# Modulation vectors on VectorE beside two products, and the first layer's output, norm and queries tile by tile

## The chip, the core and the metric

The kernel runs on one core of a Trainium2 chip, as one program. The metric is device time in microseconds (us); the time before is the median of three runs. Within the core TensorE (PE) multiplies matrices into PSUM, VectorE (DVE), ScalarE (ACT) and GpSimd (POOL) work on SBUF and PSUM, and SyncE (SP) issues loads. Every engine runs its own queue in order; they wait for each other on semaphores. Sixteen DMA engines carry all transfers of the core.

## The reference

All values are float32. There are 256 tokens of width 1024, in two tiles of 128. A first block has two layers, each a mixer, an output product with residual and norm, and a feed-forward part that fetches 128 experts a token (8 heads, 16 each). A second block has two layers, each with a modulation vector.

```python
# first block, layer i
x = layer_norm(DN_ALPHA * x + mix @ w_out[i], ln1_g[i], ln1_b[i])
q = x @ peer_w_q[i]                       # 8 heads, 2 halves of 128
s = q . subkeys                           # 128 keys a half, top 16 of each, top 16 of the 256 sums
y = sum over the 16 chosen experts of 8 heads: softmax(sums) * gelu(u_tab[e] . x) * v_tab[e]
x = layer_norm(DN_ALPHA * x + y, ln2_g[i], ln2_b[i])
# second block
c_act = silu(c)
for l in range(2):
    mod = c_act @ w_ada[l] + b_ada[l]     # 1024 -> 3072
    shift, scale, gate = split(mod, 3)
    h = rms_norm(x, norm_g[l]) * (1 + scale) + shift
    x = x + gate * (attention_parts(h @ w_in[l]) @ w_o[l])
```

## The kernel before

**Weights.** All large weights pass through a ring of three slots (`RING = 3`). SyncE issues the loads in the order in which `weights.add` was called (L2730); load n waits until half 1 of product n-3 is done (`half_done[1]`). A group of 512 columns is two DMAs of 1.05 MB. A product's two halves go to the PSUM banks `bank(slot, half)` and wait for `bank_read` of the product that used them before.

**Stages.** Code is cut into stages; `meet` drains TensorE, ScalarE and VectorE and lets each wait for the others.

**The first layer** (`mlstm_layer`). One stage makes the gate, memory and query/key products on TensorE (`qk`, four groups of 384 columns) while VectorE runs the gates: `log1p_steps`, the scans, `exp_reduce`. After cross-attention the decay stage follows: for each of 4 heads TensorE makes scores, VectorE the decay exponents, ScalarE the exponentials. Layer 0's modulation vector is made in this stage on TensorE: `partial_sums` (L855) multiplies a group of w_ada with silu(c) in four column groups, ScalarE copies the partial sums, `full_sum` adds them by ones and adds the bias (L869, L870), ScalarE copies the row. Then come the normalised output `ro`, `residual_product` with w_out for both tiles (L302, L936), `layer_norm_stage` for both tiles and `x_transposes`, each a stage of its own.

**The expert stream** (`middle`). A table of slots sets the order: 4 tiles (2 layers of 2) of 128 slots. A slot is one gather of 128 expert rows of 8 KB (L2361, GpSimd), one dot product (L1864, VectorE), its gelu, coefficient and diagonal (ScalarE, by pairs), and one addition on TensorE (L1758, eight instructions). Eight rows are in flight: gather n waits for addition n-8. Everything else is placed between slots by numbers that `beside()` yields: on TensorE the queries of heads 4 to 7, the memory products, layer 1's modulation vector (slots 62 to 106, w_ada's six groups), and layer 1's mixer; on VectorE the ranking of the chosen experts in pieces (`route`), which `plan_chunk` places. Ahead of slot 0 stand the queries of heads 0 to 3 (`queries(0, h)`, 256 columns, both tiles at once), the key products, the ranking of head 0 and most of head 1's. `order` and `homes` give every side job its PSUM bank.

**After the stream**, in its last stage, `second_layer(0)` makes `rv_`, `rz`, `rq` and `rk` from w_in, ten groups of 512 columns, and goes on to the attention.

Of the kernel before, what the change touches and what calls it, by code (L numbers as in the profile page):

```python
# [169 lines left out]
def program(nc, a, out, parts=None):  # L170
# [27 lines left out]
    c_col = sb([P, KD], name="silu_c")  # L198
    c_wide = sb([P, KD, 32], name="silu_c_and_zeros")
# [46 lines left out]
    norm_loaded, rg_loaded = sig("norm_gain_and_shift_landed"), sig("gate_matrices_landed")  # L246
    mod_cols_in, sums_read = sig("modulation_columns_landed"), sig("expert_sums_read")
# [243 lines left out]
    def load_mod_cols(act):  # L491

        act.wait_ge(mod_stored.sem, 16 * DEPTH)
        with nc.allow_non_contiguous_dma("small parameters"):
            for layer in range(DEPTH):
                act.dma_start(mod_cols[:, layer, 0, :], a["norm_g_2"][layer].rearrange("(k p) -> p k", p=P))\
                    .then_inc(mod_cols_in.sem, 16)
                for i in range(2):
                    act.dma_start(mod_cols[:, layer, 1 + i, :],
                                  a["mod_scratch"][layer][i * D:(i + 1) * D].rearrange("(k p) -> p k", p=P))\  # L500
                        .then_inc(mod_cols_in.sem, 16)

    def mod_gains(dve):

        dve.wait_ge(mod_cols_in.sem, 16 * 3 * DEPTH)
        for layer in range(DEPTH):
            chains["vector"](dve.scalar_tensor_tensor(
                out=mod_cols[:, layer, 0, :], in0=mod_cols[:, layer, 2, :], scalar=1.0, in1=mod_cols[:, layer, 0, :],
                op0=ALU.add, op1=ALU.mult))
# [238 lines left out]
    def setup_pool(pool):  # L748
# [7 lines left out]
        p(pool.memset(c_wide[:, :, :], 0.0))  # L756
# [21 lines left out]
    def setup_scalar(act):  # L778
# [4 lines left out]
        act.activation(c_wide[:, :, 0], c_col[:, :], ACT.Silu)  # L783
# [41 lines left out]
    class Modulation:  # L825


        def __init__(self, layer):
            self.layer = layer
            self.row = sb([1, 3 * D], name="mod_row")  # L830
            self.part = sb([P, 2, 512], name="mod_partial")
# [5 lines left out]
        def add_weights(self):  # L837
            self.run = weights.add([(a["w_ada_2"][self.layer], 0, P, KD)], 0, 512, 6)

        def place(self, g):  # L840
            n = self.run.first + g
            return n, n % RING, n // RING

        def partial_sums(self, pe, g):
            n, slot, turn = self.place(g)
            w = weights.view(slot, KD, 512)

            pe.wait_ge(landed[slot].sem, (turn + 1) * 32)
            if g >= 1:
                before, s, t = self.place(g - 1)  # L850

                pe.wait_ge(bank_read[s][0].sem, t + 1)
            for k in range(KD):
                j = k % 4
                last = pe.matmul(psum[32 * j:32 * j + 32, 6, :], c_wide[:, k, :], w[:, k, :], start=k < 4, stop=k >= 4)  # L855
            last.then_inc(half_done[0].sem, 1)

        def full_sum(self, pe, g):
            n, slot, turn = self.place(g)

            pe.wait_ge(bank_read[slot][0].sem, turn + 1)
            if g >= 1:
                before, s, t = self.place(g - 1)

                pe.wait_ge(bank_read[s][1].sem, t + 1)
            else:

                pe.wait_ge(bias_landed.sem, self.need)
            pe.matmul(psum[0:1, 7, :], ones[:, 0:1], self.part[:, g % 2, :], start=True, stop=False)  # L869
            pe.matmul(psum[0:1, 7, :], ones[0:1, 0:1], self.row[:, g * 512:(g + 1) * 512], start=False, stop=True)\  # L870
                .then_inc(half_done[1].sem, 1)
# [336 lines left out]
    def middle():  # L1208
# [567 lines left out]
        def vector(dve):  # L1776
# [298 lines left out]
            for _ in experts_norm(5, 3, 0):  # L2075
                pass
# [724 lines left out]
```

## Time and profile before

| | |
|---|---|
| median of 3 runs | 2686.25 us (2684.17 to 2686.85) |
| the profiled execution | 2687.56 us, span 2685.7 us |
| mean granted clock of TensorE | 0.885 |
| busy: PE, DVE, ACT, POOL | 78%, 50%, 27%, 22% of the span |
| read from HBM | 745.64 MB |
| first gather, last gather issued | 285.00, 1769.57 us |

The busy shares are means over parts with different limits, so they say little by themselves. The page's slices (67 us each) show the parts, and the timeline gives start, length, engine, line and tiles, with the idle time before a row and what ended it in brackets. "x16" is a number of instructions; a float32 product on TensorE is two. A window row gives its length, the busy time of each engine with its instructions, the granted clock (1.00 is 2.4 GHz, 0.50 is 1.2 GHz), the mean busy share of the DMA engines and GB/s; with a line as filter only that line's engine is shown.

### The profile page before, as it was taken

What the parts mean: (1) busy time and instruction counts of PE and PEld (TensorE: products, weight loads), DVE (VectorE), ACT (ScalarE), POOL (GpSimd) and SP (SyncE); (2) the same over time, 40 slices, a digit from 0 to 9 for tenths busy, and PEclk for the clock granted to TensorE, in tenths of its full rate; (3) what the DMA queues carried; (4) which work ended last, traced back from release to release, by engine and by line L of the source; (5) the groups of instructions that cost most, each with busy time, mean ns of one, the idle gap of its engine ahead of it and who ended that gap; (6) DMA issues with size and microseconds to landing.
All of it is one profiled execution on the core that took longest, in us unless ns stands there. A gap on an engine that the chain in (4) does not pass through costs nothing. (4 is left out here: it accounts for less than half of the span.)

```text
span 2685.7 us, 29026 instructions
## 1 busy us (share of the span) xinstructions
PE 2084.0 (78%) x10382; PEld 1082.4 (40%) x10382; DVE 1344.5 (50%) x3611; ACT 730.7 (27%) x2078; POOL 590.3 (22%) x530
## 2 busy tenths in 40 slices
PE   7987777676676776677685456669998999999897
PEld 5644423111243342243251111126864544875553
DVE  3143686666778546787556867540024322012432
ACT  0120233233335322344323233320032410022230
POOL 0000344334433433334333344510000000000000
PEclk9999899777887898888797788779999999999899
DMA  5354799999999999999998999974413143430331
GB/s 174 133 204 145 291 416 419 420 418 417 416 380 392 409 419 416 367 387 399 414 420 343 391 402 421 421 317 157 151 38 135 35 157 131 151 120 29 119 115 63
DMA packets 209159, 748.67 MB, mean 279 GB/s; under 512 B 29764, under 2 KB 69700, under 8 KB 143476
## 3 DMA queue, kind: packets, MB, share of 16 engines
q0 software_dynamic: 73728, 536.90, 48.9%
q1 hardware_dynamic: 111120, 195.35, 20.5%
q10 hardware_dynamic: 24168, 14.57, 1.9%
q8 instruction: 83, 1.36, 0.2%
q14 instruction: 60, 0.49, 0.0%
HBM read 745.64 MB, written 1.12 MB: 278 GB/s over the span
## 5 line engine op out<-in xcount | busy, mean ns | idle before, releaser
L1758 PE MATMUL psum<-expert_rows,coefs_on_diagonal 64*64 64x512 f32 x4096 | 660.3, 751 | 486.5 <-ACT coefs_on_diagonal L2145 486.1
L2361 POOL DMA_INDIRECT expert_rows<-in_peer_uv,expert_ids x512 | 585.5, 1144 | 1179.0 <-PE psum L1758 859.9
L1864 DVE SCALAR_TENSOR_TENSOR expert_rows<-expert_rows,x 128x1024 f32<-128x1024 f32 x512 | 626.5, 1225 | 412.5 <-DMA expert_rows<-in_peer_uv,expert_ids 407.7
L1758 PEld LDWEIGHTS psum<-expert_rows,coefs_on_diagonal 64*64 64x64 f32 x4096 | 141.7, 155 | 835.2 <-ACT coefs_on_diagonal L2145 655.3
L2135 ACT ACTIVATE gelu_dots<-dots 128x2 f32<-128x2 f32 x256 | 52.0, 203 | 939.7 <-DVE expert_rows L1864 900.9
L302 PE MATMUL psum<-xT,ring 128*128 128x256 f32 (+2 forms) x1088 | 237.2, 381 | 2.1 <-DVE bias_rows L715 2.1
L575 PE MATMUL psum<-ring,xT 128*128 128x512 f32 (+2 forms) x448 | 217.6, 585 | 0.0
L302 PEld LDWEIGHTS psum<-xT,ring 128*128 128x128 f32 (+2 forms) x1088 | 196.6, 181 | 44.3 <-DVE bias_rows L715 3.7
L2145 ACT ACTIVATE coefs_on_diagonal<-ident,coefs 128x128 f32<-128x128 f32 x512 | 177.5, 393 | 8.4
L1465 PEld LDWEIGHTS psum<-xT,ring 128*128 128x128 f32 x768 | 109.3, 197 | 84.4 <-issue 79.2
L1465 PE MATMUL psum<-xT,ring 128*128 128x128 f32 (+1 forms) x768 | 142.4, 330 | 0.6 <-DVEq L2705 0.6
L2138 ACT ACTIVATE coefs<-gelu_dots,gate_weights 128x1 f32<-128x1 f32 x512 | 123.0, 287 | 8.5
L664 ACT ACTIVATE prob<-soft,small 128x128 f32<-128x128 f32 (+1 forms) x96 | 53.9, 561 | 170.4 <-DVE small L632 154.8
L2410 PE MATMUL psum<-ring,xT 128*128 128x512 f32 x192 | 86.2, 610 | 7.8 <-DVE x L1897 4.1
L575 PEld LDWEIGHTS psum<-ring,xT 128*128 128x128 f32 x448 | 72.8, 194 | 29.5 <-issue 21.3
L302 PE MATMUL psum<-ring,xT 128*128 128x512 f32 (+1 forms) x192 | 78.4, 568 | 5.2 <-DVE num L1144 3.3
L1559 PEld LDWEIGHTS psum<-xT,ring 128*96 128x96 f32 x512 | 59.2, 167 | 41.3 <-issue 41.3
L1559 PE MATMUL psum<-xT,ring 128*96 128x128 f32 x512 | 69.7, 286 | 0.0
L2410 PEld LDWEIGHTS psum<-ring,xT 128*128 128x128 f32 x192 | 37.3, 196 | 55.8 <-issue 51.7
L2458 DVE SCALAR_TENSOR_TENSOR ya<-psum,small,silu_az 128x64 f32<-128x64 f32 x32 | 9.1, 284 | 98.0 <-PE psum L587 98.0
L2640 PE MATMUL psum<-ring,mergedT 128*128 128x512 f32 x128 | 55.6, 594 | 2.8 <-DVEq L2705 1.4
L2438 DVE COPY da_qT<-psum 128x512 f32<-128x512 f32 x6 | 4.1, 691 | 106.2 <-PE psum L302 106.2
(449 smaller groups left out, 2284.5 us busy)
## 6 DMA issues: line engine op xcount, KB each, us to landing
ring<-in_w_in SPq DMA_DIRECT2D x64, 1024.0 KB, 7.1
ring<-in_w_ada SPq DMA_DIRECT2D x24, 1024.0 KB, 12.7
ring<-in_peer_w_q SPq DMA_DIRECT2D x24, 1024.0 KB, 28.5
ring<-in_mlstm_w_in SPq DMA_DIRECT2D x16, 768.0 KB, 5.1
ring<-in_rglru_w_in SPq DMA_DIRECT2D x16, 768.0 KB, 26.4
expert_rows<-in_peer_uv,expert_ids POOLq DMA_INDIRECT x512, 14.4
ring<-in_w_out_b SPq DMA_DIRECT2D x8, 1024.0 KB, 7.2
ring<-in_w_o SPq DMA_DIRECT2D x8, 1024.0 KB, 5.9
```

The lines of the kernel that those rows point to most:

```text
L302: last = pe.matmul(o, l, r, start=first, stop=end)
L575: ins = pe.matmul(o, l, r, start=first, stop=end)
L664: act.activation(prob[:, j % 2, 0:w], soft[:, j % 2, 0:w], ACT.Exp, bias=small[:, 0, at4(j)], accum_out=small[:, 1, at4(j)]).then_inc(expe ...
L1465: last = pe.matmul(out[:, s * wide:(s + 1) * wide], w[:, kt, at:at + P], right[:, kt, :], start=kt == 0, stop=kt == KD - 1)
L1559: last = pe.matmul(out[0:RG_B, b * P:(b + 1) * P], w[:, kt, at:at + RG_B], xT[:, kt, t * P:(t + 1) * P], start=kt == 0, stop=kt == KD - 1)
L1758: last = pe.matmul(psum[64 * half:64 * half + 64, 2 * t + m, :], diag[tokens, n % DIAGS, tokens], rows[tokens, at_, D + half * 512:D + (ha ...
L1864: dve.scalar_tensor_tensor(out=rows[:, at_, 0:D], in0=rows[:, at_, 0:D], scalar=1.0, in1=x[:, n // TILE % NT, :], op0=ALU.mult, op1=ALU.mu ...
L2138: ins = act.activation(coef[:, at_ + q:at_ + q + 1], gel[:, at_ + q:at_ + q + 1], ACT.Copy, scale=gw[:, g_at:g_at + 1])
L2145: ins = act.activation(diag[:, (s + q) % DIAGS, :], ident[:, :], ACT.Copy, scale=coef[:, at_ + q:at_ + q + 1])
L2361: pool_.indirect_dma_start(out=rows[:, n % ROWS, :], out_offset=None, in_=table, in_offset=bass.IndirectOffsetOnAxis(ap=ids[:, at_:at_ + 1 ...
L2410: last = pe.matmul(o, l, r, start=first, stop=end)
L2640: last = pe.matmul(o, l, r, start=first, stop=end)
```

## The change

Modulation is no longer made by products on TensorE. `multiply` lets VectorE take a group of w_ada from the ring: a `tensor_scalar` for k = 0 and seven `scalar_tensor_tensor`, each adding `w[:, k, :] * silu(c)[:, k]` to `acc` [128, 512]. `reduce` adds the 128 partitions of `acc` on TensorE with a column of ones, in two products of 256 columns, and `add_bias` adds the row on VectorE. Layer 0's six groups move from the decay stage into the query/key stage, one between every two of its products. Layer 1's six groups leave the stream and stand between the six `rq` and `rk` groups of the stage after it. `load_mod_cols` and `mod_gains` are done for each layer apart.

The output product of the first layer, its norm, and the transposes now are part of the stream's stage. `out_product(pe, t)` makes both groups of w_out for one tile. VectorE adds the residual and norms tile 0 while TensorE makes tile 1's product. `queries(0, h)` for both tiles become `pair_queries(c, t)`: two heads of one tile, four blocks of 128 columns in one bank. Ahead of slot 0 stand tile 0's heads 0 to 3; tile 1's x is turned at slot 0, and the other six pairs follow in slots 4 to 45, five matmuls a slot.

Cut to its core, the diff:

```diff
@@ Modulation
+        def multiply(self, dve, g):
...
+            dve.wait_ge(landed[n % RING].sem, (n // RING + 1) * 32)
+            if g >= 2:
+
+                dve.wait_ge(half_done[1].sem, self.at[g - 2] + 1)
+            v(dve.tensor_scalar(acc, w[:, 0, :], c_act[:, 0:1], None, ALU.mult))
+            for k in range(1, KD):
+                ins = dve.scalar_tensor_tensor(out=acc, in0=w[:, k, :], scalar=c_act[:, k:k + 1], in1=acc,
+                                               op0=ALU.mult, op1=ALU.add)
...
+        def reduce(self, pe, g):
...
+            pe.wait_ge(mod_summed.sem, self.first + g + 1)
+            for half in range(2):
+                if n >= RING:
+
+                    pe.wait_ge(bank_read[n % RING][half].sem, n // RING)
+                pe.matmul(bank(n % RING, half)[0:1, 0:256], ones[:, 0:1], self.acc[:, g % 2, half * 256:half * 256 + 256],
+                          start=True, stop=True).then_inc(half_done[half].sem, 1)
@@ mlstm_layer, tensor
+            mod.reduce(pe, 0)
+            product(pe, kvj)
+            for i in range(4):
+                mod.reduce(pe, i + 1)
+                product(pe, [(qk[i], "features", x_k, [(0, 0, 0, 96), (0, T, 96, 96), (1, 0, 192, 96), (1, T, 288, 96)])])
+            mod.reduce(pe, 5)
@@ mlstm_layer, vector
             v(dve.tensor_tensor(lf[:, :], z[:, :], lf[:, :], ALU.subtract))
+            mod.multiply(dve, 2)
+            mod.add_bias(dve, 1)
@@ decay stage
-                for g in mod_groups[h]:
-                    mod.partial_sums(pe, g)
-                    mod.full_sum(pe, g)
@@ end of the first layer
-        residual_product([(a["w_out"][layer], 0, P, KD)], 512, lambda k: mixT[:, k, :])
-        layer_norm_stage(gain, shift, dict(scalar=lambda act: act.wait_ge(mod_stored.sem, mod.stored)))
-        x_transposes()
@@ middle, tensor ahead of slot 0
-            all_of(queries(0, 0))
+            out_product(pe, 0)
...
-            second = queries(0, 1)
+            out_product(pe, 1)
+            turn_x(0)
+            x_read(0)
+            out_read(pe)
+            all_of(pair_queries(0, 0, (0, 1), ("q0",)))
+            second = pair_queries(0, 0, (2, 3))
...
-            all_of(queries(0, 2))
-            all_of(queries(0, 3))
+            all_of(pair_queries(1, 0))
@@ middle, tensor beside()
-                for g in range(6):
-                    yield 62 + 8 * g
-                    partial_modulation(g)
-                    yield 66 + 8 * g
-                    full_modulation(g)
@@ middle, vector ahead of the ranking
+            for t in range(NT):
+                for g in range(2):
+                    residual(dve, g, t)
+                    norm_stats(t, g)
...
+                for _ in norm(t, t, 0):
+                    pass
@@ second_layer
+            for i, (run, dst, first) in enumerate(rqk):
+                if mod:
+                    mod.reduce(pe, i)
+                product(pe, [(run, "features", x_k, four)])
```

How the change moves instructions, at three places.

TensorE in the query/key stage, before (`xT` is the layer's input turned, `memT` the memory, `ring` the weights):

```order
L302 MATMUL psum<-xT_69,ring_67 128x256 x16
L302 MATMUL psum<-memT_70,ring_67 128x256 x16
L302 MATMUL psum<-ring_67,memT_70 128x256 x16
L302 MATMUL psum<-xT_69,ring_67 96x256 x128
L560 MATMUL psum<-kmT_99,xqT_98 128x256 x2
```

and now:

```order
L303 MATMUL psum<-xT_69,ring_67 128x256 x16
L867 MATMUL psum<-mod_partial_sums_112,ones_50 1x256 x2
L303 MATMUL psum<-memT_70,ring_67 128x256 x16
L303 MATMUL psum<-ring_67,memT_70 128x256 x16
L867 MATMUL psum<-mod_partial_sums_112,ones_50 1x256 x2
L303 MATMUL psum<-xT_69,ring_67 96x256 x32
L867 MATMUL psum<-mod_partial_sums_112,ones_50 1x256 x2
L303 MATMUL psum<-xT_69,ring_67 96x256 x32
```

The `reduce` products stand between the groups, and what follows each on TensorE waits behind it.

TensorE from the output product to slot 0, before (`mixT` is the mixer's output turned, `peer_qT` the queries):

```order
L302 MATMUL psum<-ring_67,mixT_125 128x512 x32
L336 MATMUL psum<-ident_49,x_68 128x128 x16
L1465 MATMUL psum<-xT_69,ring_67 128x256 x16
L1729 MATMUL psum<-ident_49,subkeys 128x128 x4
L1465 MATMUL psum<-xT_69,ring_67 128x256 x4
L1519 MATMUL psum<-subkeysT_152,peer_qT_153 128x128 x2
L1465 MATMUL psum<-xT_69,ring_67 128x256 x12
L1519 MATMUL psum<-subkeysT_152,peer_qT_153 128x128 x2
L1465 MATMUL psum<-xT_69,ring_67 128x256 x32
```

and now:

```order
L1211 MATMUL psum<-ring_67,mixT 128x512 x16
L1756 MATMUL psum<-ident_49,subkeys 128x128 x4
L1211 MATMUL psum<-ring_67,mixT 128x512 x16
L1561 MATMUL psum<-ident_49,x_68 128x128 x8
L1516 MATMUL psum<-xT_69,ring_67 128x128 x20
L1549 MATMUL psum<-subkeysT_143,peer_qT_144 128x128 x2
L1516 MATMUL psum<-xT_69,ring_67 128x128 x12
L1549 MATMUL psum<-subkeysT_143,peer_qT_144 128x128 x2
L1516 MATMUL psum<-xT_69,ring_67 128x128 x32
```

Ahead of the first key product there are now 8 transposes and 20 products of 128 columns, where there were 16 and 20 of 256.

VectorE in the query/key stage behind the gates' log (`log_f`), where before `cum_f` followed at once, now:

```order
L1012 TENSOR_TENSOR log_f_92<-ml_z_90,log_f_92 4x256
L850 TENSOR_SCALAR mod_partial_sums_112<-ring_67,silu_c_57 128x512
L852 SCALAR_TENSOR_TENSOR mod_partial_sums_112<-ring_67,silu_c_57,mod_partial_sums_112 128x512 x7
L882 TENSOR_TENSOR mod_row_111<-mod_row_111,psum 1x256 x2
L1015 SCALAR_TENSOR_TENSOR cum_f_93<-ones_50,log_f_92 4x256
L1016 TENSOR_TENSOR a_94<-gate_i_87,cum_f_93 4x256
```

Group 2's multiplication and the bias row of group 1 stand between two steps of the gates.

## Rows read from the trace of the kernel before

Timeline rows: start in us, length in us, engine, line, operation, written tile, read tiles, shapes, number of instructions, and in brackets the idle time before and what ended it. Window rows: stretch, length, busy time of each engine shown (with its instructions), granted clock, DMA share, GB/s.

**Rows 1.** Page, part 2: DMA engines, 40 slices, busy tenths
```profile
DMA  5354799999999999999998999974413143430331
```

**Rows 2.** Windows of the gathers' line (slots 48 to 111; 432 to 495)
```profile
411.30:607.60 196.30, 69.83 (x64) 0.78 1.02 419
...
1573.90:1734.40 160.50, 75.92 (x64) 0.78 1.01 421
```

**Rows 3.** Timeline of SyncE: start, length, engine, line, operation, tiles
```profile
418.25 74.92 SPq L2730 DMA_DIRECT2D ring<-in_w_ada  x8
...
517.67 27.45 SPq L2730 DMA_DIRECT2D ring<-in_w_ada  x4
...
568.00 177.39 SPq L2730 DMA_DIRECT2D ring<-in_rglru_w_in  x10
```

**Rows 4.** Timeline, query/key stage and its end
```profile
54.67 55.42 PE L302 MATMUL psum<-xT,ring 128*96 128x256 f32 x256
...
65.50 0.68 DVE L1005 TENSOR_TENSOR_SCAN cum_f<-ones,log_f 4x256 f32<-4x256 f32 x1
...
110.79 1.13 PE L560 MATMUL psum<-kmT,xqT 64*128 64x256 f32 x4 [0.71 <-ACTq L2705]
```

**Rows 5.** Timeline, decay stage and the stage behind it
```profile
146.74 2.93 PE L1072 MATMUL psum<-qkT 96*128 96x256 f32 x8 [0.51 <-DVEq L2705]
...
149.47 0.56 DVE L356 SCALAR_TENSOR_TENSOR decay_t<-decay_turns,decay_t 128x384 f32<-128x384 f32 x1
...
150.73 0.86 DVE L1085 SCALAR_TENSOR_TENSOR decay_t<-psum,a_and_floor_columns,causal_t 128x256 f32<-128x256 f32 x2
...
153.08 1.02 PE L869 MATMUL psum<-mod_partial,ones 128*1 128x512 f32 x2 [0.72 <-ACT mod_partial L880]
...
154.03 1.01 PE L870 MATMUL psum<-mod_row,ones 1*1 1x512 f32 x2
...
156.04 0.87 DVE L1085 SCALAR_TENSOR_TENSOR decay_t<-psum,a_and_floor_columns,causal_t 128x256 f32<-128x256 f32 x2
...
183.38 4.19 PE L1126 MATMUL psum<-v_and_ones,p_t 128*128 128x193 f32 x24 [1.21 <-ACTq L2705]
```

**Rows 6.** Timeline, output product and the first query read
```profile
217.81 27.73 PE L302 MATMUL psum<-ring,mixT 128*128 128x512 f32 x64 [1.42 <-ACTq L2705]
...
271.59 0.59 ACT L2091 COPY peer_qT<-psum 128x512 f32<-128x512 f32 x1 [20.04 <-issue]
```

**Rows 7.** Timeline, first ranking to gather 8
```profile
273.44 0.29 DVE L1797 MAX8 best_scores<-key_scores 128x8 f32<-128x128 f32 x1 [4.52 <-ACT key_scores L2105]
...
285.00 1.09 POOL L2361 DMA_INDIRECT expert_rows<-in_peer_uv,expert_ids  x1 [278.33 <-DVE expert_ids L1838]
...
296.06 0.18 DVE L1852 TENSOR_TENSOR gate_exp<-gate_exp,gate_power 128x16 f32<-128x16 f32 x1 [10.44 <-ACT gate_exp L364]
...
305.63 1.22 DVE L1864 SCALAR_TENSOR_TENSOR expert_rows<-expert_rows,x 128x1024 f32<-128x1024 f32 x1
...
311.33 3.69 PE L1758 MATMUL psum<-expert_rows,coefs_on_diagonal 64*64 64x512 f32 x16 [15.22 <-ACT coefs_on_diagonal L2145]
...
313.62 1.64 POOL L2361 DMA_INDIRECT expert_rows<-in_peer_uv,expert_ids  x1 [18.84 <-PE psum L1758]
```

**Rows 8.** Windows at the stream's start
```profile
285.00:320.00 35.00, 19.05 (x95) 11.94 (x93) 21.28 (x68) 11.05 (x30) 12.05 (x12) 0.76 0.80 312
...
310.00:315.00 5.00, 3.67 (x17) 0.85 (x17) 4.80 (x15) 3.53 (x14) 1.38 (x1) 0.50 0.13 45
```

**Rows 9.** Timeline of TensorE in tile 1: six products, one addition (8 instructions)
```profile
961.12 1.60 PE L1465 MATMUL psum<-xT,ring 128*128 128x128 f32 x12
...
963.93 1.09 PE L1758 MATMUL psum<-expert_rows,coefs_on_diagonal 64*64 64x512 f32 x8 [1.21 <-ACT coefs_on_diagonal L2145]
```

**Rows 10.** Stage after the stream: TensorE's timeline, and a window
```profile
1856.00 83.04 PE L302 MATMUL psum<-xT,ring 128*128 128x256 f32 x384
...
1856.00:1864.00 8.00, 8.00 (x39) 7.04 (x38) 0.00 (x0) 1.18 (x2) 0.00 (x0) 1.00 0.74 262
```

More of the change, by code:

```diff
@@ L837, in add_weights @@
         def add_weights(self):
[L838 to L871, printed above, removed]
+            g = len(self.at)
@@ L874, in load_bias, with add_bias @@
             act.dma_start(self.row[:, :], row(a["b_ada_2"][self.layer], 1, 3 * D)).then_inc(bias_landed.sem, 16)
-        def read_partial(self, act, g):
-            n, slot, turn = self.place(g)
-            act.wait_ge(half_done[0].sem, n + 1)
-            act.copy(self.part[:, g % 2, :], psum[:, 6, :]).then_inc(bank_read[slot][0].sem, 1)
-        def read_sum(self, act, g):
-            n, slot, turn = self.place(g)
-            act.wait_ge(half_done[1].sem, n + 1)
-            act.copy(self.row[:, g * 512:(g + 1) * 512], psum[0:1, 7, :]).then_inc(bank_read[slot][1].sem, 1)
+        def add_bias(self, dve, g):
+            n = self.at[g]
+            if g == 0:
+                dve.wait_ge(bias_landed.sem, self.need)
+            for half in range(2):
+                dve.wait_ge(half_done[half].sem, n + 1)
+                cols = slice(g * 512 + half * 256, g * 512 + half * 256 + 256)
+                dve.tensor_tensor(self.row[:, cols], self.row[:, cols], bank(n % RING, half)[0:1, 0:256], ALU.add)\
+                    .then_inc(bank_read[n % RING][half].sem, 1)
@@ L997, in vector @@
             exp_reduce(dve, v, e[:, :], gkf[:, :], gki[:, :]).then_inc(to_act.sem, 1)
+            mod.multiply(dve, 1)
+            mod.add_bias(dve, 0)
             kv_dve(dve)
@@ L1033, in scalar @@
             exp_rest(act, c, z2[:, :]).then_inc(to_dve.sem, 1)
-            read_both(act, qk, lambda g, half, b: act.copy(qkT[:, bass.ds(g * 4 + 2 * half, 2), :], two(b, 96)))
+            for i in range(4):
+                read_both(act, qk[i], lambda g, half, b, i=i: act.copy(qkT[:, 4 * i + 2 * half:4 * i + 2 * half + 2, :],
+                                                                       two(b, 96)))
+            mod.store(act)
         stage(tensor=tensor, vector=vector, scalar=scalar)
@@ L2387, in second_layer @@
         rz = weights.add([(w, 0, P, KD)], 4608, 512, 1)
-        rq = weights.add([(w, 0, P, KD)], 0, 512, 3)
-        rk = weights.add([(w, 0, P, KD)], 1536, 512, 3)
+        mod = None
+        if layer == 0:
+            attend_at, place[0] = place[0], ya_end + 8 * 1024
+            mod = Modulation(1)
+            place[0] = attend_at
+        rqk = []
+        for i in range(6):
+            if mod:
+                mod.add_weights()
+            rqk.append((weights.add([(w, 0, P, KD)], i * 512, 512, 1), qT if i < 3 else kT, i % 3 * 4))
         x_k = lambda k: xT[:, k, :]
@@ L2422, in scalar @@
             read_both(act, rz, lambda g, t, b: act.activation(az[:, t, :], b, ACT.Silu))
-            for run, dst in ((rq, qT), (rk, kT)):
-                read_out(act, 0, run, lambda g, b: act.copy(dst[:, bass.ds(g * 4, 2), :], two(b)))
+            for run, dst, first in rqk:
+                read_out(act, 0, run, lambda g, b: act.copy(dst[:, first:first + 2, :], two(b)))
+            if mod:
+                mod.store(act)
+                load_mod_cols(act, 1)
         turned_at = 4 * layer
```

328 lines of the change are left out of this document (180 added, 148 removed).

## The prediction

> **What bounds the kernel now.** I read the page's slices first: from slice 6 to slice 26 of 40 the DMA row stands at 9, and outside that stretch it is mostly at 5 or below [rows 1]. So the program has three parts with two bounds: before the expert stream TensorE and its waits, in the stream the 16 DMA engines, after it TensorE again. Next I counted gathers: 64 of them took 196.3 us in slots 48 to 111 and 160.5 us in slots 432 to 495, at the same granted clock (0.78) and the same DMA share [rows 2]. The reader is to see that no engine's instructions set this pace: what differs is what else the DMA engines carry. In the slow stretch they carry the 12 loads of w_ada, 1.05 MB each [rows 3].
>
> **Stream without w_ada.** The excess is 196.3 - 160.5 = 35.8 us. The first two of the next row, 1.05 MB together, fall there too, so w_ada's part is 12.58 / 13.63 of it: 33.0 us. Bounds: 12.58 MB at 421 GB/s [rows 2] is 29.9 us; the whole excess is 35.8. I take 33. TensorE's modulation products go with it, but nothing waited on them there.
>
> **Modulation of layer 0, in the query/key stage.** TensorE runs 256 matmuls from 54.67 to 110.09 without a gap, and the next stage starts at 110.79 [rows 4]. Now six `reduce` steps stand between its products, two 256-column products of one row each. The nearest rows are the 512-column ones, which start 0.95 us apart [rows 5]; two of half the width: 0.95 us a step, 5.7 us in all. VectorE multiplies before each step: one tensor_scalar and seven scalar_tensor_tensor over 512 columns. The row for 384 columns is 0.56 us at a pitch of 0.59 [rows 5]; scaled to 512 with the fixed part kept it is 0.69 at 0.72, so one group costs 7 x 0.72 + 0.45 = 5.5 us (the tensor_scalar is an estimate, bounds 0.3 and 0.72). Is it in time? Walking the order with these durations: group 0 is multiplied while TensorE is still in the stage's first product. TensorE wants it at 40.9 (54.67 less two memory products of 6.9). Group 1's load is let go by `reduce` 0 at 42 behind 1 MB of memory values, lands near 50.5, is multiplied by 56, its bank is freed by `add_bias` 0 (two instructions of about 0.4 us) at 56.8: 0.8 us late. Group 2 stands behind the log1p polynomial, which in the trace ends before the scan at 65.50 [rows 4] and now ends 2.5 us later; 68.0 + 5.5 = 73.5 against 71.7: 1.8 us late. Groups 3 to 5 each have a product of 13.8 us in front of them and need 8 us for the load and 5.5 for the multiply: in time. At the end `add_bias` and the store are 1.2 us longer than the copy they replace. Sum +9.5 us; bounds +5.7 (nothing late) and +14.
>
> **Layer 0's decay stage loses its modulation.** It lasts from 146.74 until TensorE's next stage at 183.38 [rows 5]. What is left is VectorE's chain: one head every 156.04 - 150.73 = 5.3 us where modulation doesn't hold it. Four heads and the last wait for ScalarE end near 168.5, the next stage at 169.4: -14.0 us (bounds -12 and -15). ScalarE now also waits for the row's store there, issued some 25 us before.
>
> So the output product of layer 0, at S = 217.81 before [rows 6], starts at about 213.3.
>
> **Output, norm and queries by tile.** Before: product 27.7 us, norm, transposes, `q` of head 0, a wait for ScalarE, which issued parameter loads and could read that `q` only at 271.59, key product, ranking from 273.44 = S + 55.6, first gather at 285.00 = S + 67.2 [rows 6, 7]. After: tile 0 is normed beside tile 1's product. S + 28.3 product and transposes of keys done; tile 0's x turned by S + 30.2; ScalarE's copies come behind `root(1)`, S + 31.8; 16 products of 128 columns S + 35.4; copy, key product, copy: ranking from S + 37.7. VectorE has finished tile 1's norm at S + 33.7. First gather S + 49.3: -17.9 us. Where a stall goes, what is late next? VectorE's wait for `gate_exp`, 10.4 us at 296.06 [rows 7]: in ScalarE's queue it stood behind two full query reads. Now one read stands there (S + 48), before VectorE asks at S + 50. So the first dot moves from S + 87.8 [rows 7] to S + 61.7, and gather 8, which needs the first addition, from S + 95.8 to S + 69.7. The eight gathers ahead occupy DMA 8 x 2.5 = 20 us from S + 49.3, so no hole is left; before, DMA was idle 20% of 285 to 320 = 7.0 us, most of it after 310 [rows 8]. -7.0 us (bounds -4 and -7).
>
> What this moves into the saturated stretch: the fourth group of peer_w_q (2.1 MB), earlier loaded before the first gather, now released in slot 11; at 33.0 / 12.58 = 2.62 us per MB, +5.5. The gain and shift of ln2, 1.05 MB, now loaded at slot 80: +2.6 (at 2.39 to 2.62 per MB).
>
> TensorE in slots 4 to 45: per slot now 4.6 products of 128 columns instead of 2 of 256. Six cost 1.60 us, an addition 1.09 [rows 9], so 1.2 to 1.35 + 1.05 = 2.3 to 2.4 us against DMA's 2.51 per slot. Nearly bound; I put 3 us for it (bounds 0 and 12).
>
> **Modulation of layer 1, in the first stage after the stream.** TensorE is gapless there [rows 10]; six steps of 0.95 add 5.7, the store and column loads fit behind the last half product of 6.9 us: +6 (bounds +5.5 and +12). The margin: a group of 2.1 MB is in within 8 us of its release [rows 10] (262 GB/s x 8 us), plus 5.5 us is 13.5, and 14.8 are there. Behind the waiting `reduce` stands the next query/key product and the rest of the stage.
>
> **Sum** against the profiled execution's 2687.56: +9.5 - 14.0 - 17.9 - 7.0 - 33.0 + 5.5 + 2.6 + 3 + 6 = -45.3. The small column loads, three of six, leave the stream: -1 to -3, I take 1.5. Total -46.8: 2640.8. The median of the runs shown is 1.3 below the profiled execution: **2639.5 us**.
>
> **Rivals.** (A) Late multiplications; the one that ends slower. Place: `reduce` 3 to 5 of layer 0 and 1 to 5 of layer 1, with a group's load sharing the DMA engines with the one issued 1 us behind it. Both then land only after 4.2 MB, some 12.5 us: 18 against 14.8, 3.2 us late at each of 8 steps, 26 us. It becomes slower than before only if each wait also lets TensorE's clock fall: after its wait before 311.33 the granted clock was 0.50 (1.2 GHz) and 16 instructions took 3.69 us instead of 2.1 [rows 7 to 9]. A product of 13.8 us half of it at this clock costs 6.9 more, 8 x 6.9 = 55: 2639.5 + 26 + 55 = 2720. It decides from where load plus multiply exceeds 14.8 us by enough to drop the clock; against it, the wait in the row was 15.22 us, not 3, and the margin is positive. 4%. The Trainium skill (TensorE: Matmul & The Clock Gate, section "HAM oscillation — how this bites in real kernels") speaks for it: it tells of a kernel in which every short wait for a load makes the next products start on the low clock. It also says, in DMA: Bandwidth & Descriptors, section "Queues, rings and completion order", that the descriptors that SyncE issues are taken in ring order on each DMA engine, by which the second load would not delay the first and the stall would be nothing. No row of before has two such loads close together, so none shows which holds.
> (B) TensorE sets the pace in slots 4 to 45: 2.8 us a slot in place of 2.51 is 12 us, so 2639.5 + 9 = 2649, up to 2655. For it: 2.3 to 2.4 is close, and additions come in pairs; against it, in the trace TensorE makes up such slots in the next ones while rows are still queued. 16%.
> (C) The stream doesn't give back the bytes: slots 48 to 111 were slow because ranking and landing latency (eight rows in flight) set the pace. Then about half of 33 us stays: 2656. Against it: same clock and share in both rows [rows 2]. 7%.
> (D) All bounds on the good side, and w_ada worth 35.8: 2630. 9%.
> The forecast itself, 2631 to 2649: 64%.
>
> **Range and chances.** 8 in 10 is held by the forecast, D's upper part and most of B: 2627 to 2656. A measurement of this kernel tells about 0.2% (5 us) from no change. Only A, with 4%, is slower; no change would need several misses at once, 1%; faster 95%.
>
> **What would show each step.** Next profile: `reduce` rows idle under 2 us each; decay stage about 22 us long; first gather near 262; gather 8 within 21 us of gather 0, with DMA share near 1 from there; slots 48 to 111 in about 161 to 166 us; the stage after the stream 6 us longer. Wrong if `reduce` waits grow beyond 3 us with clock 0.5 behind them, or if slots 48 to 111 still take over 180 us.

## The result, and the profile after

The changed kernel takes 2650.11 us (median of 4 runs, 2645.83 to 2656.59), the kernel before 2685.21 in the same set. The ratio is 0.9871, with an interval of 0.985 to 0.9893. In two later sets it was 0.9855 (0.9838 to 0.9872) and 0.9861 (0.9839 to 0.9884). The median of all twelve runs is 2648.0. So the change is faster by 35 to 40 us in the three sets. The forecast was 2639.5: the direction and the range held, and the time is 8 to 11 us above the forecast.

The executions of the changed kernel spread over 14 us, wider than most of its single terms. So I place its three profiled executions side by side (span 2654.8, 2645.8 and 2646.2 us) and take a term as real only where all three agree. Times in us, gathers counted from 0:

| stretch | before | after, three executions | forecast |
|---|---|---|---|
| start to output product (S) | 217.8 | 223.4, 217.2, 217.9 | 213.3 |
| S to gather 0 | 67.2 | 48.7, 50.3, 48.7 | 49.3 |
| gather 0 to 48 | 126.4 | 125.8, 125.2, 125.8 | 127.9 |
| gather 48 to 112 | 196.3 | 175.5, 176.1, 175.5 | 161 to 166 |
| gather 112 to 496 | 1126.8 | 1125.5, 1123.4, 1124.7 | 1125.3 |
| gather 496 to the end | 951.3 | 956.0, 953.5, 953.7 | 957 |

The join by tiles (second line) came as forecast. Two lines miss: the start, by 4 to 10 us, and gathers 48 to 112, by 10 us even against the upper end of the forecast (165.9, with the gain and shift of ln2, is what the sum used). The column before is one execution, and its start is a favourable one: two experiments below that have the old instructions in this part reach S at 221.2 and 222.5.

Page of the changed kernel, part 2 and one queue of part 3 (packets, MB, share of 16 engines); it answers to [rows 1]:

```profile
PEclk8979898677988696888797778789999999999999
DMA  6614899999999999999999999957714044430331
...
q0 software_dynamic: 73728, 536.90, 49.8%
```

The saturated stretch now runs from slice 5, at 8 tenths, to slice 26 (of 66 us each). All 512 gathers are queue q0: 1.05 MB each.

Windows of the gathers' line in the changed kernel (length, POOL busy with its instructions, granted clock, DMA share, GB/s), which answer to [rows 2]:

```profile
397.83:573.30 175.47, 71.49 (x64) 0.79 1.02 417
1538.80:1698.80 160.00, 74.19 (x64) 0.82 1.01 421
272.10:397.80 125.70, 54.04 (x48) 0.89 1.00 405
```

Same rate (417 and 421 GB/s), different length: the two differ by the bytes carried. The first row (slots 48 to 111) is 15.5 us longer than the second (64 later slots), where I had expected 1 to 6.

SyncE in the changed kernel, which answers to [rows 3]:

```profile
336.13 39.18 SPq L2782 DMA_DIRECT2D ring<-in_xattn_w_kv  x4
411.14 42.80 SPq L2782 DMA_DIRECT2D ring<-in_rglru_w_in  x6
689.36 17.57 SPq L2782 DMA_DIRECT2D ring<-in_rglru_w_in  x4
```

w_ada is gone, but six loads of the next weights now start between 411 and 454, in its place. Before, the row of ten such loads began at 568 and reached behind slot 112.

TensorE in the changed kernel, from the query/key stage to the first addition; it answers to [rows 4, 5, 6 and 7]:

```profile
42.58 1.02 PE L867 MATMUL psum<-mod_partial_sums,ones 128*1 128x256 f32 x4
43.54 7.17 PE L303 MATMUL psum<-memT,ring 128*128 128x256 f32 x32
50.55 7.07 PE L303 MATMUL psum<-ring,memT 128*128 128x256 f32 x32
60.89 1.02 PE L867 MATMUL psum<-mod_partial_sums,ones 128*1 128x256 f32 x4 [3.27 <-DVE mod_row L882]
...
125.22 1.13 PE L559 MATMUL psum<-kmT,xqT 64*128 64x256 f32 x4 [1.12 <-ACTq L2757]
...
160.38 4.55 PE L1091 MATMUL psum<-qkT 96*128 96x256 f32 x16 [0.51 <-DVEq L2757]
...
182.25 7.22 PE L1139 MATMUL psum<-v_and_ones,p_t 128*128 128x193 f32 x24 [4.31 <-ACTq L2757]
192.74 23.83 PE L303 MATMUL psum<-ring,xT 128*128 128x384 f32 x64 [3.27 <-DVE num L1157]
...
223.42 14.00 PE L1211 MATMUL psum<-ring,mixT 128*128 128x512 f32 x32 [0.58 <-DVEq L2757]
...
289.11 1.99 PE L1789 MATMUL psum<-expert_rows,coefs_on_diagonal 64*64 64x512 f32 x8 [16.26 <-ACT coefs_on_diagonal L2186]
```

Sum 1 waits 3.27 us. The decay stage (160.38 to 182.25) is 21.9 us long, as forecast. The stage behind it took 4.19 us before [rows 5] and takes 7.22 now. Windows of TensorE there and in the gate's products behind (length, busy time with its instructions, granted clock, DMA share, GB/s) show the lower of the clock's two levels, 1.2 GHz; before, 183.4 to 187.5 had a granted clock of 1.00:

```profile
182.30:188.00 5.70, 5.70 (x18) 0.50 0.00 0
192.80:198.40 5.60, 5.60 (x9) 0.50 0.00 1
```

GpSimd and VectorE of the changed kernel, which answer to [rows 7]:

```profile
260.51 0.29 DVE L1828 MAX8 best_scores<-key_scores 128x8 f32<-128x128 f32 x1 [3.48 <-ACT key_scores L2146]
...
272.06 1.09 POOL L2388 DMA_INDIRECT expert_rows<-in_peer_uv,expert_ids  x1 [265.77 <-DVE expert_ids L1869]
...
291.40 0.94 POOL L2388 DMA_INDIRECT expert_rows<-in_peer_uv,expert_ids  x1 [9.41 <-PE psum L1789]
```

Gather 8 starts 19.3 us after gather 0, where it took 28.6 before; within the 21 us forecast. In the 35 us from gather 0 the mean DMA share is 0.94, where it was 0.80 [rows 8].

### The profile page after: what moved, and what is told of

It is laid out like the page before. It is cut to its first block and busy times, and to the rows that moved or that the text cites. A ratio compares the mean times of both kernels' runs of the same rounds, so it can differ in the third digit from the quotient of the medians.

```text
span 2654.8 us, 29228 instructions
## 1 busy us (share of the span) xinstructions
PE 2059.5 (78%) x10446; PEld 1102.9 (42%) x10446; DVE 1419.8 (53%) x3729; ACT 721.1 (27%) x2060; POOL 602.7 (23%) x529
## 5 line engine op out<-in xcount | busy, mean ns | idle before, releaser
L1789 PE MATMUL psum<-expert_rows,coefs_on_diagonal 64*64 64x512 f32 x4096 | 672.2, 765 | 480.7 <-ACT coefs_on_diagonal L2186 480.3
L2388 POOL DMA_INDIRECT expert_rows<-in_peer_uv,expert_ids x512 | 598.2, 1168 | 1132.6 <-PE psum L1789 831.9
L574 PEld LDWEIGHTS psum<-ring,xT 128*128 128x128 f32 x448 | 73.0, 195 | 29.5 <-issue 21.3
L1504 PEld LDWEIGHTS psum<-xT,ring 128*128 128x128 f32 x512 | 64.0, 200 | 41.4 <-issue 41.4
L1516 PEld LDWEIGHTS psum<-xT,ring 128*128 128x128 f32 x512 | 63.3, 199 | 38.1 <-issue 35.5
L1516 PE MATMUL psum<-xT,ring 128*128 128x128 f32 x512 | 71.8, 292 | 2.4 <-ACT xT L2195 2.4
L1504 PE MATMUL psum<-xT,ring 128*128 128x128 f32 x512 | 73.4, 294 | 0.0
L852 DVE SCALAR_TENSOR_TENSOR mod_partial_sums<-ring,silu_c,mod_partial_sums 128x512 f32<-128x512 f32 x84 | 63.1, 752 | 3.0
```

The source lines that it names most:

```text
L574: ins = pe.matmul(o, l, r, start=first, stop=end)
L852: ins = dve.scalar_tensor_tensor(out=acc, in0=w[:, k, :], scalar=c_act[:, k:k + 1], in1=acc, op0=ALU.mult, op1=ALU.add)
L1504: last = pe.matmul(out[:, s * P:(s + 1) * P], w[:, kt, at:at + P], xT[:, kt, (k - 1) * P:k * P], start=kt == 0, stop=kt == KD - 1)
L1516: last = pe.matmul(out[:, b * P:(b + 1) * P], w[:, kt, b * P:(b + 1) * P], xT[:, kt, t * P:(t + 1) * P], start=kt == 0, stop=kt == KD - 1)
L1789: last = pe.matmul(psum[64 * half:64 * half + 64, 2 * t + m, :], diag[tokens, n % DIAGS, tokens], rows[tokens, at_, D + half * 512:D + (ha ...
L2388: pool_.indirect_dma_start(out=rows[:, n % ROWS, :], out_offset=None, in_=table, in_offset=bass.IndirectOffsetOnAxis(ap=ids[:, at_:at_ + 1 ...
```

## The experiments

Each was timed in five rounds beside the kernel before; intervals are those of the ratio.

**Control** (the changed kernel, once in each of two sets).

> The changed kernel once more, the control of this set. Its profiled execution was 6.5 us above its median (2656.6 against 2650.1). Theory 1 (the stages' differences against the forecast are real): TensorE's stage after the emptied decay stage again takes about 7 us in place of 4, the products of the output gate 23.8 us in place of 20.9, slots 48 to 111 take 173 to 178 us; only the stretch behind slot 112 may come out shorter. Theory 2 (the profiled execution was a bad draw): these three come out near 4, 21 and 166 us, and the span is 6 us shorter by that.

> The changed kernel as control of this set: 2647 to 2650, ratio 0.9855 to 0.987; first gather at 267 to 272 us.

Measured: 2646.77 us, 0.9855; and 2648.03 us, 0.9861. TensorE of the first control:

```profile
180.45 6.54 PE L1139 MATMUL psum<-v_and_ones,p_t 128*128 128x193 f32 x24 [4.30 <-ACTq L2757]
190.26 20.88 PE L303 MATMUL psum<-ring,xT 128*128 128x384 f32 x64 [3.27 <-DVE num L1157]
```

The slow stage behind the decay stage is real (7.2, 6.5, 5.6 us in three executions). The gate's products are not: 23.8, 20.9, 22.6 us with the same 3.27 us of waiting in front. Slots 48 to 111 are real. So theory 1 holds in two of its three parts.

**Layer 0's modulation back on TensorE.**

```diff
-        mod = Modulation(layer // 2 * 2)
+        mod = ModulationOnTensor(layer // 2 * 2)     # the class of the kernel before
         ...                                          # six sums leave the query/key stage
                 last.then_inc(scored.sem, 1)
+                for g in mod_groups[h]:
+                    mod.partial_sums(pe, g)
+                    mod.full_sum(pe, g)
```

> The changed kernel with layer 0's modulation again on TensorE in the decay stage. Theory 1: the move cost 14.4 us in the query/key stage, gave 14.8 in the decay stage, and lost 6.0 behind it to the lower TensorE clock; undoing it gives 5.6 us: 2644.5 against 2650. Theory 2 (the forecast's own terms, +9.5 and -14.0, hold on the median): undoing it costs 4.5 us: 2654.5.

Measured: 2653.98 us, 0.9886 (0.987 to 0.9903) against the control's 0.9855: 7 us slower. My theory 1 fell, the forecast's terms stand. I had read S of one bad execution (223.4). In this run, with the same instructions as before in that part, S is 221.2, against 217.8 before, since its stage behind (granted clock 0.50 from 183.0 to 185.5) and its gate's products drew a low clock too:

```profile
182.93 5.63 PE L1195 MATMUL psum<-v_and_ones,p_t 128*128 128x193 f32 x24 [1.23 <-ACTq L2814]
191.84 22.57 PE L304 MATMUL psum<-ring,xT 128*128 128x384 f32 x64 [3.27 <-DVE num L1213]
```

**Clock held in the decay stage.** Products whose result nothing reads, 16 and then 7 per head.

```diff
                 last.then_inc(scored.sem, 1)
+                for _ in range(16):       # the second run: 7
+                    pe.matmul(psum[:, 6, 0:T], ident[:, :], ones[:, :], start=True, stop=True)
```

> The changed kernel with 16 products of 256 columns per head added in the decay stage, whose results nothing reads, so that TensorE does not idle there. Theory 1: the stage behind falls from 7.2 to about 4.2 us and the gate's products from 23.8 to about 21 us, at granted clock near 1.0: 2644 against 2650, the decay stage itself stays at 21.9 us. Rival: the slow products there come from something else (operands, the load of the weights), and the time stays at 2650, or rises if the added products delay the scores of the next head.

> The changed kernel with 7 products of 256 columns per head added in the decay stage (0.44 us each as measured with 16 of them: 3.1 us in the 3.8 that TensorE has free per head); nothing reads their results. Theory 1 (the idle decay stage lowers TensorE's clock for the stage behind it): that stage falls from 6.5 to 7.2 us back to 4.2, the decay stage stays at 21.9: 2644 against 2646.8 of the control. Rival: the clock is down for another reason there, or the added products delay the next head's scores: no gain, 2647 to 2650.

Measured: 2659.03 us (0.9906, 0.9893 to 0.992) and 2650.64 us (0.9869, 0.985 to 0.9888). Sixteen products take 7.07 us per head, more than the idle time, and lengthen the stage to 36.5 us; I had sized them wrongly. Seven fit. TensorE of that run:

```profile
174.34 3.19 PE L1095 MATMUL psum<-ones,ident 128*128 128x256 f32 x14
180.11 4.19 PE L1141 MATMUL psum<-v_and_ones,p_t 128*128 128x193 f32 x24 [2.59 <-ACTq L2759]
187.57 20.88 PE L303 MATMUL psum<-ring,xT 128*128 128x384 f32 x64 [3.28 <-DVE num L1159]
```

The stage behind is back at 4.19 us, as in the run with sixteen products and in the last version below: a filled decay stage keeps the clock up there in all three. But the emptying alone doesn't explain the low clock. With the old modulation in the decay stage the stage behind took 4.19 us in one execution and 5.63 and 5.87 in two others (layer 0's modulation back on TensorE; bytes alone):

```profile
182.73 5.87 PE L1126 MATMUL psum<-v_and_ones,p_t 128*128 128x193 f32 x24 [1.20 <-ACTq L2706]
```

With the decay stage emptied it took 5.60 to 7.22 us in eight executions. The means are 5.2 and 6.4 us: the emptying costs some 1.2 us on average, and 1.4 to 3.0 only against the one execution before. The gate's products don't follow the decay stage: with sixteen products in it they took 22.57 us. With seven, S is 214.6 and gather 0 comes at 264.8, 2.7 us ahead of the first control. Still the whole is not faster: behind gather 496 this execution takes 958.4 us where the controls take 953.6.

**Modulation alone** (both layers on VectorE, no join by tiles).

```diff
         rv = weights.add([(a["xattn_w_kv"][1], 0, P, KD)], XA_W, XA_W, 1)
-        mod.add_weights()
         ...                    # the stream's partial and full sums, their reads and the store go;
         ...                    # query/key stage and first stage after the stream as in the change
```

> The kernel before with the modulation part alone (both layers on VectorE, in the query/key stage and in the first stage after the stream), without the join by tiles. Theory 1: +14.4 -14.8 +6.0 for layer 0, 12.58 MB out of the stream at the 2.38 us per MB of the DMA engines' 421 GB/s: -30 at most and -24 if the stretch behind slot 112 gives nothing back, +4.3 after the stream: -14 to -20, so 2665 to 2671. By the forecast's terms (+9.5 -14.0 -33.0 -1.5 +6): 2652. Rival C (the stream gives back half of the bytes' time): 2676 to 2680.

Measured: 2664.77 us, 0.9925 (0.991 to 0.9939): -20.7 us of the whole, and the join is worth the other 18. That is the edge of what theory 1 said (2665 to 2671), 13 us above the forecast's terms (2652) and 11 below the nearer end of rival C. From gather 0 to gather 496 it takes 1420.6 us, before 1449.5: -28.8 for 12.58 MB. Its window of slots 48 to 111 (and the first of the next):

```profile
408.80:581.10 172.30, 73.10 (x65) 0.82 1.02 418
```

**Bytes alone.** The kernel before; layer 1's w_ada loads bring 8 of 128 partitions, and the modulation's instructions stay.

```diff
+                        if getattr(run, "thin", False):      # layer 1's w_ada
+                            sp.dma_start(view[p0:p0 + 8, k0:k0 + k, :], src[0:8, :, bass.ds(col + col0, run.cols)])\
+                                .then_inc(landed[slot].sem, 16)
+                            continue
```

> The kernel before, in which layer 1's twelve w_ada loads in the stream bring 8 of the 128 partitions (11.8 MB less); TensorE's and ScalarE's modulation instructions stay in place, on stale weights. If bytes alone set the price at the rate of the modulation-only run (28.9 us for 12.58 MB, 2.30 us per MB): -27, 2658. By the forecast's 2.62 us per MB: -31, 2654.5. Rival C (ranking, TensorE and ScalarE pace half of that stretch): -14, 2671.

Measured: 2666.22 us, 0.9926 (0.9911 to 0.994): -20.7 on medians. Its trace has -22.9 us from gather 0 to 496. The window of slots 48 to 111:

```profile
415.20:593.00 177.80, 69.81 (x65) 0.85 1.01 397
```

The rate has fallen to 397 GB/s: 177.8 us x 397 is 70.6 MB, which at 421 would take 168. My reading was that TensorE's modulation products and their handshakes hold the additions up, now that the bytes are gone, and that this costs the 6 us (28.8 - 22.9) by which the run above is better. Shorter windows of the same trace don't bear that out:

```profile
422.00:432.00 10.00, 5.45 (x4) 0.89 1.02 367
432.00:452.00 20.00, 6.86 (x8) 0.88 1.01 419
452.00:462.00 10.00, 4.30 (x5) 1.00 1.01 359
...
512.00:522.00 10.00, 4.70 (x5) 0.84 1.02 360
```

The rate falls to 351 to 370 GB/s in the six stretches of 10 us behind the six pairs of reduced loads, and up to the last pair it is 419 to 422 between them, at a DMA share of 0.98 to 1.02 in both. Against 421 GB/s the six lack some 8.5 us, more than the 6. Additions that hold the gathers up would leave the DMA engines idle, as between 310 and 315 us before, at a share of 0.13 [rows 8]; here the share stays. So what slowed this run goes with the reduced loads themselves, which means with my edit; why a load into 8 partitions does this, no run shows. What is left is that 11.8 MB gave 22.9 us at least, where the rate alone would give 28. That TensorE's instructions have a part in the slow stretch is not shown, and rival C (14 us) falls.

**Sums over partitions in the decay stage.**

```diff
-                pe.matmul(bank(n % RING, half)[0:1, 0:256], ones[:, 0:1], self.acc[:, g % 2, ...])
+                pe.matmul(bank(n % RING, half)[0:1, 0:1], ones[:, 0:1], ones[:, 0:1])   # frees the slot
...
+            pe.matmul(psum[0:1, 6 + g % 2, :], ones[:, 0:1], self.sums(g))   # per head, decay stage
```

> The changed kernel; layer 0's six sums over partitions (0.95 us each on TensorE) move from the query/key stage, where a product of 1 column stays to release the ring's slot, into the idle time of TensorE in the decay stage; the bias is added in the partial sums, ScalarE copies. Theory: six times 0.65 us less in the query/key stage, 1 us less at its end (no store behind it), and up to 2.5 us less behind the decay stage if the clock holds: 2641 to 2643 against 2646.8. Rival: what costs there is not the products but TensorE's handshakes with VectorE and the late group 1, and the added sums and copies lengthen the decay stage: 2647 or more.

Measured: 2653.32 us, 0.9875 (0.9857 to 0.9894), against the control's 0.9855: nothing gained. TensorE:

```profile
59.57 0.24 PE L924 MATMUL psum<-ones 128*1 128x1 f32 x4 [4.08 <-DVE mod_crumb L931]
...
77.13 0.24 PE L924 MATMUL psum<-ones 128*1 128x1 f32 x4 [1.65 <-DVE od_partial_sums_more L915]
...
107.60 0.24 PE L924 MATMUL psum<-ones 128*1 128x1 f32 x4 [2.09 <-DVE od_partial_sums_more L915]
```

The step is 0.78 us shorter, 4.7 us in all, but TensorE now waits 7.8 us for VectorE in place of 3.5 to 4.0, and the low clock behind two of these waits takes the rest (15.7 us for a product of 14.05). The cadence is set by when VectorE is through, not by the sum.

**Multiply when the first half is in,** alone, then with the late sums, then with the clock held too (3 products per head, 7 at the last).

```diff
-            dve.wait_ge(landed[n % RING].sem, (n // RING + 1) * 32)
+            dve.wait_ge(first_landed[n % RING].sem, self.early[g])
             v(dve.tensor_scalar(acc, w[:, 0, :], c_act[:, 0:1], None, ALU.mult))
             for k in range(1, KD):
+                if k == KD // 2:
+                    dve.wait_ge(landed[n % RING].sem, n // RING * 32 + 16)
```

> The changed kernel; each w_ada group's two loads count on separate semaphores, and VectorE multiplies the first four row blocks when the first half is in, so after the second half only four steps of 0.78 us are left in place of eight. Theory (TensorE waits in the query/key stage because load, 8 to 10.6 us, plus multiplication, 6.0 us, is as long as the 14.95 us between two sums): the wait before sum 1 falls from 3.1 us to under 0.5, those of 0.2 to 0.7 us go, the product behind sum 1 takes 14.05 in place of 15.7: the next stage starts 4 to 5 us earlier, 2642 to 2644 against 2647 to 2650. Rival: both halves land together, since the DMA engines share them, and nothing is gained: the wait stays at 3 us.

> The same with layer 0's sums over partitions in the decay stage. Late sums alone gained nothing, since TensorE then waited 4.1, 1.7 and 2.1 us for VectorE. Theory: with the multiplication early these waits go, and the six products that are 0.78 us shorter now count: another 4 to 5 us, 2638 to 2640. Rival: the load itself is the cadence (landing 8 to 9 us after its release, and 3.9 us of steps behind it, against 14.2 us between two steps is not tight), so if waits remain they come with VectorE's other work (log1p) in front: no gain over the version above.

> The same with 3 products of 256 columns behind the sums of heads 0 to 2 and 7 behind head 3, to hold TensorE's clock over the end of the decay stage. Theory: the stage behind takes 4.2 us in place of 6.5 to 7.1: 2.5 us earlier first gather; of the whole, 2636 to 2638, unless the lower clock later in the program takes it back as in the run with held clock alone (its first gather was 2.7 us earlier, its end was not). Rival: the products delay the next head's scores, and the decay stage grows by the same.

Measured: 2647.73 (0.9854), 2646.95 (0.9853) and 2646.20 us (0.9851), each interval about 0.983 to 0.9875, against the control's 0.9861. All three expectations (2642 to 2644, 2638 to 2640, 2636 to 2638) were too low. TensorE and VectorE of the first:

```profile
58.04 1.02 PE L876 MATMUL psum<-mod_partial_sums,ones 128*1 128x256 f32 x4 [0.56 <-DVE mod_row L891]
...
69.11 0.49 DVE L856 TENSOR_SCALAR mod_partial_sums<-ring,silu_c 128x512 f32<-128x512 f32 x1
...
75.17 1.48 PE L876 MATMUL psum<-mod_partial_sums,ones 128*1 128x256 f32 x4 [2.12 <-DVE mod_partial_sums L860]
```

The wait before sum 1 fell from 3.1 to 0.56 us. But multiplication 2 begins at 69.11, without idle time before it: it stands behind the log1p polynomial, and sum 2 now waits 2.12. The wait moved to the next one in VectorE's queue. The third version's gather 0 comes at 262.6, 4 us before the control's 266.6, yet its gather 496 only 2.0 us before, and its end is level. No version is measurably faster than the changed kernel.

**Layer 1's modulation left out.**

```diff
-            mod = Modulation(1)
+            mod = NoSums(1)        # loads and stores the bias row, nothing else
```

> The changed kernel with layer 1's modulation left out (no loads of w_ada, no multiplications, no sums; the stored row is the bias). The forecast's term for it is 6 us, the modulation-only run's trace has 6.6 us more behind the last gathers: 2640 to 2641 against 2646.8. Rival: VectorE's multiplications delay the reads of the query and key products, and it is worth 10 or more: below 2637. Other rival: the six steps hide in the stage, 2646.

Measured: 2639.16 us, 0.983 (0.9812 to 0.9847), 7.6 us below the control. The stage itself shows the price more closely than the end of the program does. TensorE in the kernel before, then in the changed kernel, from the first sum to the next stage:

```profile
1939.87 2.23 PE L560 MATMUL psum<-da_kT,da_qT 64*128 64x128 f32 x12 [0.83 <-DVEq L2705]
...
1821.18 1.02 PE L867 MATMUL psum<-mod_partial_sums,ones 128*1 128x256 f32 x4
...
1912.13 2.23 PE L559 MATMUL psum<-da_kT,da_qT 64*128 64x128 f32 x12 [0.83 <-DVEq L2757]
```

Before, the six groups took 83.9 us (from 1856.00 [rows 10] to 1939.87), and they take 83.9 in this run. With the modulation they take 90.95, 91.08 and 91.04 us in the three executions: +7.1. Six sums at 0.95 us are 5.7 of it, the last wait 0.2 to 0.3, and the rest is that a product cut off by sums takes some 0.2 us more than one in an unbroken row. The other rival (the steps hide) and the first (10 us or more) both fall.

## Why the forecast was right, and what it missed

**Query/key stage, +9.5: too small.** From the start of its first product to the next stage it was 85.5 us before (25.32 to 110.79) and 99.6, 97.8 and 98.8 after: +12.3 to +14.1. Up to 1.4 us of this is not the change's: the first product, ahead of every sum, took 15.4 to 17.0 us in the three and 15.5 before. The six sums cost 0.95 us each, as said. What was mis-sized is "group 1: 0.8 us late". SyncE and VectorE of the changed kernel:

```profile
42.69 0.92 SPq L2782 DMA_DIRECT2D ring<-in_xattn_w_kv  x2
43.65 1.05 SPq L2782 DMA_DIRECT2D ring<-in_w_ada  x2
...
54.30 0.49 DVE L850 TENSOR_SCALAR mod_partial_sums<-ring,silu_c 128x512 f32<-128x512 f32 x1 [7.74 <-DMA ring<-in_w_ada]
54.82 5.47 DVE L852 SCALAR_TENSOR_TENSOR mod_partial_sums<-ring,silu_c,mod_partial_sums 128x512 f32<-128x512 f32 x7
```

The load is issued at 43.65, 1 us behind the memory values, and is in only at 54.3: 10.65 us, not 8. A multiplication takes 6.0 us (seven steps at 0.78), not 5.5. Together 3.3 us late, and behind this wait a product of 14.05 us takes 15.7 in two of the three executions and 14.65 in the third, where the sum ahead of it took 1.86 us instead of 1.02. Group 2 was 0.4 to 0.7 us late, not 1.8. The margin for the later groups (13.5 against 14.8) was thin: in one execution group 4 took 9.05 us to load and 6.0 to multiply, against 14.95 from sum to sum, and in the others about 8 and 6.0.

**Rival A** came true at none of its eight steps (in the changed kernel they wait 0.3 us at most), but its mechanism did at sum 1, and with it one of the forecast's own signs of being wrong: a wait of 3.1 to 3.3 us, with a granted clock of 0.54 from 61.84 to 65.50 behind it. That cost about 5 us, not 26 and 55. The rival's 12.5 us for 4.2 MB (336 GB/s) goes by no row. Waits of 0.2 to 0.7 us left the next product at 14.05 us, in other runs waits of up to 1.65 us too, while behind waits of 2.1 to 4.1 us it took 14.7 to 16.7. The Trainium skill (TensorE: Matmul & The Clock Gate, "HAM oscillation — how this bites in real kernels") tells of a kernel whose waits for loads, as long as this one or longer, each let the next products start on the low clock; the trace agrees for the 3.3 us, and of waits under 1 us the section says nothing. Of the order on the DMA engines, two loads 1 us apart in the first stage after the stream show:

```profile
1821.28 0.92 SPq L2782 DMA_DIRECT2D ring<-in_w_ada  x2
1822.24 1.49 SPq L2782 DMA_DIRECT2D ring<-in_w_in  x2
...
1829.37 0.48 DVE L850 TENSOR_SCALAR mod_partial_sums<-ring,silu_c 128x512 f32<-128x512 f32 x1 [14.65 <-DMA ring<-in_w_ada]
```

The first is in after 8.1 us although the second follows at once, as long as w_ada's loads with nothing behind them took in the query/key stage (8.0); group 1, itself the second, took 10.65. By the rule of the Trainium skill (DMA: Bandwidth & Descriptors, "Queues, rings and completion order"), which I had weighed against the rival, descriptors are taken in ring order on each DMA engine, and the trace agrees; I hadn't turned the rule on group 1, which stands behind another load.

**Decay stage, -14.0: right** (-14.8; 21.9 us in all three). What the forecast lacked is the next line: the length up to "the next stage at 169.4" was right, but TensorE enters that stage at the low clock, 1.4 to 3.0 us against the execution before and some 1.2 on average. Undoing the whole move costs 7 us against the forecast's 4.5, within what the two intervals leave open.

**Join by tiles, -17.9: right** (-16.9 to -18.5). The wait for `gate_exp` went as said, and gather 8 follows. In the stream the join was to cost +4.1 (7.0 gained by the hole, 5.5, 2.6 and 3 lost). The three executions have 1426.7, 1424.7 and 1426.0 us from gather 0 to 496, the modulation alone 1420.6: +4.1 to +6.1. Of the hole, the share of 0.94 leaves some 2.1 us idle in 35, so about 4.9 of the 7.0 came back. The other terms I can't confirm one by one. Rival B's place, gathers 0 to 48, is no slower than before (125.2 to 125.8 against 126.4) at DMA share 1.00: TensorE costs nothing there that can be seen.

**Stream without w_ada, -33: the term that was mis-sized.** Measured -28.8 in the run with the modulation alone. I had divided the excess of 35.8 us by 13.63 MB. The row itself [rows 2] tells the bytes: 196.30 us x 419 GB/s is 82.2 MB, less 67.1 for 64 gathers leaves 15.1. So a MB costs 2.4 us, which is just the rate of 421 GB/s, and 12.58 MB are 29.9, the bound that I wrote down and didn't take. What I hadn't counted is a second pair of the next weights, issued at 592.7, before slot 112, at 0.79 MB each (issue row of the kernel before, window 590 to 600: number, KB each, us to landing):

```profile
ring<-in_rglru_w_in SPq DMA_DIRECT2D x2, 768.0 KB, 21.9
```

"Slots 48 to 111 in 161 to 166 us" was wrong for another reason as well: the ring's later loads move up into the place that w_ada leaves. In the changed kernel that stretch carries 73.2 MB (175.47 x 417), not 67.1, and what it carries more is missing behind slot 112. There only 1.3 to 3.4 us came back. The 1.5 us for the column loads can't be seen by themselves.

**First stage after the stream, +6: right in the main, 1.1 too small.** The stage itself is 7.1 us longer, and leaving the modulation out gives 7.6 on medians; what was missing is the 0.2 us of each product that the sums cut off. That only 2.2 to 4.7 us more stand behind gather 496 (6.6 with the modulation alone) comes from other places: behind this stage the three executions take 742 to 743 us to the end, the one before 746. I put no cause to that.

Against the mean of the three profiled executions the miss is 10.0 us: +6.2 before the output product, -0.1 in the join, +6.7 in the stream, -2.8 behind it. Part of the 6.2 is luck in the row that I started from. With the old instructions ahead of it S was 217.8, 221.2 and 222.5 in three executions (mean 220.5); with the new ones, the run without layer 1's modulation included, 223.4, 217.2, 217.9 and 216.2 (mean 218.7). I had built on the lowest of the first three, some 2.7 us below their mean. The clock's part in the rest, and in the -2.8 at the end, I can't settle.

## What to carry to other kernels

Where the DMA engines are saturated, price removed bytes by the rate of the window (length times GB/s gives what was carried), not by an excess divided by the loads you can name; and expect a ring of prefetches to move up into the gap. Work that moves under TensorE's products is free only while load plus work is shorter than the product, so look whether the load is the second in its queue. When a half idle engine is emptied further, what follows may run at the low clock: here a stage of 4.2 us took 5.6 to 7.2, though with the old work in front it took up to 5.9 too. So take the start of a sum from more than one execution where the clock moves. And an edit that shrinks loads is no clean test of bytes until its own windows show an even rate.

## What the runs showed of the hardware

TensorE's clock made equal instructions differ: 64 products of 384 columns, always behind 3.27 us of waiting, took 20.88, 22.57 or about 23.8 us, in the controls as in the experiments, with the old work in the decay stage, with none and with products that fill it. So an execution differs from the next by several us ahead of the stream alone, and gains of 2.7 and 4.0 us at gather 0, each seen in a trace, did not reach the median. What sets which value comes stays open.

A DMA share of 1.01 to 1.02 went with 417 to 421 GB/s in the stream of 8 KB rows, and in 10 us stretches behind loads into 8 partitions with 359 to 370 (351 at a share of 0.98). So the share says that the DMA engines are occupied, and only the GB/s say what they move.
